# Differential attention scores: three products of rounded parts in place of one fp32 product, from the third step on

## The reference, cut to what matters

```python
dq = rope(rmsnorm(dq.reshape(B, S, DIFF_HEADS, 2, HEAD_DIM), diff_q_norm_g[l]), pos)
dk = rope(rmsnorm(dk.reshape(B, S, DIFF_HEADS, 2, HEAD_DIM), diff_k_norm_g[l]), pos)
...
    s = jnp.einsum('bqhcd,bkhcd->bhcqk', qb, k).astype(jnp.float32) * scale
    causal = kpos[None, :] <= qpos[:, None]
    p = jax.nn.softmax(jnp.where(causal, s, -jnp.inf), axis=-1)
    a = p[:, :, 0] - lam * p[:, :, 1]
    return jnp.einsum('bhqk,bkhe->bqhe', a.astype(v.dtype), v)
```

## Time and profile before

| | us |
|---|---|
| runs | 2419.97, 2422.97, 2423.15 (median 2422.97) |
| profiled execution, its own time | 2423.33 |
| its span in the profile | 2421.6 |
| PE busy | 2408.6 |
| DVE busy | 1426.1 |
| ACT busy | 983.4 |
| POOL busy | 233.9 |

### The profile page before, as it was taken

The page is one execution under the profiler, slowest core; times in us unless marked ns, Lnnn a source line. Parts: engine busy times, 40 slices in busy tenths (PEclk is TensorE's granted clock), DMA queues, the critical chain, the costliest instruction groups (busy, mean ns, idle before and its releaser), DMA issues.

```text
span 2421.6 us, 33933 instructions
## 1 busy us (share of the span) xinstructions
PE 2408.6 (99%) x11896; PEld 1950.9 (81%) x11896; DVE 1426.1 (59%) x2836; ACT 983.4 (41%) x1710; POOL 233.9 (10%) x354
## 2 busy tenths in 40 slices
PE   9999999999999999999999999999999999999999
PEld 7877788888887887888888788788887778888887
DVE  6756436777526447677762579846647864432532
ACT  4333424333323336443331343834336852432331
POOL 0000000000001004000000042301002840000000
PEclk9999999999999999999999999999999999999999
DMA  5322233333322330333333232042222003333333
GB/s 138 87 79 77 80 99 93 95 96 95 121 96 78 95 87 10 99 99 99 95 113 96 89 98 88 19 156 73 85 79 62 1 27 96 92 99 96 96 96 104
DMA packets 278507, 210.95 MB, mean 87 GB/s; under 512 B 12228, under 2 KB 234097, under 8 KB 278385
## 3 DMA queue, kind: packets, MB, share of 16 engines
q1 hardware_dynamic: 270465, 198.64, 27.8%
q10 hardware_dynamic: 7920, 10.70, 1.3%
HBM read 207.22 MB, written 2.10 MB: 86 GB/s over the span
## 4 chain that ended last, share of the span: by engine, by line
PE 88%; DVE 4%; POOL 2%; issue 2%; POOLq 1%; ACT 1%; DVEq 1%; DMA 0%; ACTq 0%
PE PS L161 15%; PE PS L163 15%; PE PS L162 15%; PE PS L158 11%; PE PS L159 11%; PE PS L160 11%; POOL PN L1909 2%; POOLq L1911 1%; DVE WL L154 1%; PE PS L1767 1%; PE PS L1776 1%; PE PS L668 1%; PE PS L1744 1%; PE PS L2435 1%; PE PS L2617 1%
## 5 line engine op out<-in xcount | busy, mean ns | idle before, releaser
L154 DVE TENSOR_TENSOR WL<-RAW,WH 128x1024 fp32r<-128x1024 f32 x352 | 432.8, 1229 | 691.3 <-ACT WH L149 684.1
L149 ACT ACTIVATE WH<-RAW 128x1024 fp32r<-128x1024 f32 x354 | 374.7, 1059 | 963.7 <-PE PS L160 527.2
L161 PE MATMUL PS<-XH,WH 128*128 128x512 f32 x1512 | 593.9, 393 | 0.4 <-DVE WL L575 0.2
L163 PE MATMUL PS<-XH,WL 128*128 128x512 f32 x1512 | 588.7, 389 | 0.0
L162 PE MATMUL PS<-XL,WH 128*128 128x512 f32 x1512 | 588.5, 389 | 0.0
L161 PEld LDWEIGHTS PS<-XH,WH 128*128 128x128 f32 x1512 | 283.9, 188 | 63.9 <-issue 3.3
L163 PEld LDWEIGHTS PS<-XH,WL 128*128 128x128 f32 x1512 | 283.8, 188 | 59.5
L162 PEld LDWEIGHTS PS<-XL,WH 128*128 128x128 f32 x1512 | 284.0, 188 | 58.5 <-issue 1.0
L158 PE MATMUL PS<-WH,XH 128*128 128x512 f32 x384 | 153.2, 399 | 1.1 <-DVE WL L154 1.1
L159 PE MATMUL PS<-WH,XL 128*128 128x512 f32 x384 | 150.5, 392 | 0.0
L160 PE MATMUL PS<-WL,XH 128*128 128x512 f32 x384 | 150.4, 392 | 0.0
(11 more groups left out here) (538 smaller groups left out, 3850.4 us busy)
## 6 DMA issues: line engine op xcount, KB each, us to landing
RAW<-in_ffn_w_up SPq DMA_DIRECT2D x88, 512.0 KB, 3.6
RAW<-in_w_in SPq DMA_DIRECT2D x60, 512.0 KB, 3.6
RAW<-in_ffn_w_down SPq DMA_DIRECT2D x44, 512.0 KB, 3.6
RAW<-in_sc_ssm_w_in SPq DMA_DIRECT2D x42, 512.0 KB, 3.7
RAW<-in_w_mlp_up SPq DMA_DIRECT2D x32, 512.0 KB, 3.9
RAW<-in_w_mlp_down SPq DMA_DIRECT2D x32, 512.0 KB, 3.6
RAW<-in_fox_w_in SPq DMA_DIRECT2D x24, 512.0 KB, 3.6
RAW<-in_sc_ssm_w_out SPq DMA_DIRECT2D x16, 512.0 KB, 3.6
```

Of the source, the lines that this page charges most:

```text
L149: act.activation(WH[:, slot, :], RAW[:, slot, :], ACT.Copy).then_inc(hi_ready, 1)
L154: dve.tensor_tensor(WL[:, slot, :], RAW[:, slot, :], WH[:, slot, :], ALU.subtract).then_inc(lo_ready, 1)
L161: pe.matmul(o, wh, ah, start=first, stop=False)
L163: return pe.matmul(o, wl, ah, start=False, stop=last)
```

## The change

From step t = 2 on, the scores are no longer fp32 products of `DQF` and `DKF` but three fp32r products: (query high, key high), (query low, key high), (query high, key low), the 128-column part included. The parts are made so:

- **Queries, high:** ACT copies tiles 2 to 7 of `DQF` to `DQH`, three after its evictions of unit 19 and three after its work of unit 20.
- **Queries, low:** POOL subtracts, six times 128x512, `DQL` over `DQF`, behind its sixteen pieces of the projection.
- **Keys:** POOL makes the high part with a tensor_scalar and the low part with a tensor_tensor, 128x512 each: for step 2 ahead of its first weights, for steps 3 to 7 each behind the weights of the step three earlier. Three buffers `DKH` take turns; `DKL` lies over `DKF`.
- PE waits ahead of step t for the six low parts of the queries and t-1 of the keys.

```diff
+    def dquery_high_act(act, tiles):
+        act.wait_ge(rd.ev, rd.at.ev + KT)
+        for t in tiles:
+            act.activation(DQH[:, t - 2, :], DQF[:, t, :], ACT.Copy).then_inc(qd.hi, 1)
+
+    def dquery_low_pool(pool):
+        for t in range(2, KT):
+            pool.wait_ge(qd.hi, qd.at.hi + t - 1)
+            pool.tensor_tensor(DQL[:, t, :], DQF[:, t, :], DQH[:, t - 2, :], ALU.subtract).then_inc(qd.lo, 1)
+
+    def dkey_parts_pool(pool, t):
+        pool.wait_ge(rd.ev, rd.at.ev + KT + t + 1)
+        pool.tensor_scalar(DKH[t % 3][:, :], DKF[:, t, :], 1.0, None, ALU.mult)
+        pool.drain()
+        pool.tensor_tensor(DKL[:, t, :], DKF[:, t, :], DKH[t % 3][:, :], ALU.subtract).then_inc(qd.lo, 1)
...
+            if n in (19, 20):
+                dquery_high_act(act, ((2, 3, 4), (5, 6, 7))[n - 19])
...
         for h in range(16):
             dunit_pool(pool, h)
+        dquery_low_pool(pool)
...
+        if t >= 2:
+            if sub == 0:
+                pe.wait_ge(qd.lo, qd.at.lo + DPARTS + t - 1)
+            pair_parts_pe(pe, da, diff_bank(t, sub), t, sub, None, None, diff_parts)
+            return
...
     def diff_pool(pool):
+        dkey_parts_pool(pool, 2)
         for t in range(KT):
...
+            if t + 3 < KT:
+                dkey_parts_pool(pool, t + 3)
```

More of the change, by code:

```diff
@@ L184, in build @@
     ex, w0s, e0, w1s, w2s, e1, w3s = (turn(early_s, half=2 * k, hi=2, lo=2) for k in (1, 0, 1, 0, 0, 1, 0))
+    DPARTS = 6
+    qd = turn(early_s, hi=DPARTS, lo=2 * DPARTS)
     qk = turn(early_s, hi=PARTS, lo=PARTS)
@@ L1721, in pair_parts_pe @@
             n = (qb + 1) * P
-            products = parts(t, qb, n) if qb else ((lambda hh: query(t, hh, qb), lambda hh: key(t, hh, n)),)
+            products = parts(t, qb, n) if qb or query is None else ((lambda hh: query(t, hh, qb), lambda hh: key(t, hh, n)),)
             for m, (q, key_) in enumerate(products):
@@ L2198, in build, with diff_parts, q_high, q_low @@
     rd = turn(rope_s, tab=2, ss=4, rt=4, rope=16, tr=16, ev=16)
+    DQH = a_("DQH", 0, [P, DPARTS, SEQ], F32R)
+    DKH = [a_("DKH0", 12, [P, SEQ], F32R), a_("DKH1", 14, [P, SEQ], F32R), a_("DKH2", 114, [P, SEQ], F32R)]
+    DQL = a_("DQL", 48, [P, KT, SEQ], F32R)
+    DKL = a_("DKL", 64, [P, KT, SEQ], F32R)
+    def dquery_high_act(act, tiles):
[11 more added lines that the diff above has]
+        pool.tensor_tensor(DKL[:, t, :], DKF[:, t, :], DKH[t % 3][:, :], ALU.subtract).then_inc(qd.lo, 1)
+    def diff_parts(t, qb, n):
+        head = [slice(HD * hh, HD * hh + HD) for hh in range(2)]
+        cols = slice(qb * P, (qb + 1) * P)
+        def q_high(hh):
+            return DQH[head[hh], t - 2, cols]
+        def q_low(hh):
+            return DQL[head[hh], t, cols]
+        def k_high(hh):
+            return DKH[t % 3][head[hh], 0:n]
+        def k_low(hh):
+            return DKL[head[hh], t, 0:n]
+        return (q_high, k_high), (q_low, k_high), (q_high, k_low)
     def diff_bank(t, sub):
```

## The result

The changed kernel takes 2432.05 us (median of 6 runs, 2431.19 to 2432.82), the kernel before 2422.23 in the same comparison (6 runs, 2419.97 to 2423.15): a ratio of 1.0043, 95% interval 1.0032 to 1.0054. It is 9.8 us slower. The forecast was 2432.5 in 2424.5 to 2437.

A forecast was written before the change was run, and what follows sets the result against it. It took the path through DVE and ACT to bound up to 1539.51, then PE, DVE and the ACT-DVE loop tied within 0.1 us. Terms 6.0+1.4-0.2+2.0-0 = +9.2 on 2423.3 gave 2432.5 us, range 2424.5 to 2437.

The forecast's parts named there:

- Scores on the path: Scores of steps 2 to 7: PE saves 0.24 to 0.44 us a step, but 0 counted on the path.
- ACT's six copies: ACT's query copies to DQH, the first three behind unit 19's evictions: covered by idle or wider cover, cost 0.
- Query lows: POOL's six query subtractions from about 1498.7 hold DVE's rotations and the ring's low part: 1.00 each, +6.0 us.
- Key parts for step 2: POOL's tensor_scalar and subtraction among the delayed rotations of pieces 13 and 14: 0.4 and 1.0, together +1.4 us.
- What absorbs it: At PE's unit 23 and its scores, waiting for the low part and then the masks: -0.2 us.
- Key parts for steps 3 to 7: POOL's subtraction holds DVE's three combines: 0.5 a period after steps 1 to 4, 0 after step 0; +2.0 us.
- rival C: PE's clock falls in the gap ahead of unit 23, some 3 us more on the path: 2435.5; chance 0.08.
- A: Rival for the stretch 1490 to 1570: POOL's work hidden, PE the bound, only PE's saving left: 2420.7; chance 0.10.
- B: Rival: POOL and DVE collisions at their low end, 3.9 for queries, nothing for keys: +3.7, 2427.0; chance 0.17.
- (1) to (3): Signs: rotations 1499 to 1510 grow about 1 us; ring's low part 6 to 8 later, PE gap 4; first exponential 7 later.
- (5): Sign in the pipeline: period near 6.9 us for steps with key parts and 6.35 without.
- (6): Sign behind 1570: the gap between the two kernels stays constant.

The follow-up runs named there:

- e1: Kernel before with only PE's part: ACT writes tiles 2 to 7 as fp32r, PE makes three products of them, no low parts; 2422.12 us, ratio 1.0000.
- e3: Kernel before, fp32 scores, with only ACT's six query copies added, no POOL subtractions; 2423.03 us, ratio 1.0003.
- e2: Kernel before, fp32 scores, with ACT's six query copies and POOL's six query subtractions added, results unread; 2428.28 us, ratio 1.0030.
- e5: Kernel before, fp32 scores, with ACT's six query copies and six one-input POOL tensor_scalars in place of the subtractions; 2423.54 us, ratio 1.0006.
- e10: Whole changed kernel with the key's high copy written as a tensor_scalar of two operations instead of one; 2430.96 us, ratio 1.0040 to the kernel before.
- e11: Changed kernel with two-operation key copy, six DKH buffers and POOL's subtractions moved to where DVE makes masks; 2425.75 us, ratio 1.0016 to the kernel before.
- e8: Kernel before, fp32 scores, with POOL's key parts added, their subtraction replaced by a second one-input tensor_scalar; 2423.40 us, ratio 1.0009.
- e9: Kernel before, fp32 scores, with POOL's key parts added, unread, the high copy written with two operations; 2425.84 us, ratio 1.0016.
- e4: Kernel before, fp32 scores, with only POOL's key parts added: six one-operation tensor_scalars and six subtractions, unread; 2425.78 us, ratio 1.0017.

## Why the prediction came out right

Point by point, by the shift:

- **Scores on the path: 0 taken, -0.1 us a period measured** (e1: 6.36 to 6.25). Right in kind. The two chains had play of 0.1. PE made a step's scores in 2.25 us instead of 2.56 (in the chain, 1.70 and 0.55 for 1.93 and 0.63), 0.31 less and inside the 0.24 to 0.44 of the forecast. The Trainium skill's four passes of true fp32 (FP8 and Floating Point Precision, TensorE Precision Notes) would make it 0.64; this trace shows half of that.
- **ACT's six copies: 0, measured 0.0** (e3).
- **Query lows: +6.0, measured +5.8** (e2). The step that carried most of the sum was right: a price taken from another two-input POOL instruction against the same rotations, plus the difference in length.
- **Key parts for step 2: +1.4, measured +1.05** (shift 5.8 to 6.87 at the first mask, 1519.49). The subtraction cost 0.9 (L2158 at 1512.98, 1.59 for 0.69), the copy 0.16 and not 0.4, in line with the 0.28 of a one-input read in e5.
- **What absorbs it: -0.2, measured 0.** The scores behind the gap ended 6.87 us late, like the masks.
- **Key parts for steps 3 to 7: +2.0, measured +3.7.** This is the mis-sized term, and it lies above its own bound of 3.2. For the parts made after step 0, where I took 0, it was +1.0; after step 1, 0; after steps 2 to 4, +0.9 each (7.24 instead of 6.36) for my 0.5. The mechanism, the subtraction on the three combines, was right. The size was off because the copy was priced at 0.76 by a tensor_scalar with two operations, and the form with one takes 1.49. That pushed the subtraction 0.7 us later, from half beside the masks to wholly beside the combines. With the short copy (e10) a period grows by 0.57, near my 0.5. For the same reason the forecast's "neither POOL nor PE's wait for the parts is late" was too easy about POOL: the pair needs 1.49+1.48 and two gaps of 0.15 to 0.19, 3.3 us and not 2.25, which is more than the 3.01 that POOL rests in a period.

The sum of the measured terms is 5.8+1.05+0+3.7-0.2 = 10.35 (the -0.2 is from the two periods without key parts), beside 9.2. That the time still came within 0.5 us of the forecast owes something to the base: I counted from a profiled execution at 2423.3, 1.1 above the median of 2422.23 that the six runs of before gave. The terms were 1.15 too low and the base 1.1 too high; that the two cancel is luck.

Two sums of the prediction don't come out. The bounds of its terms add up to +3.7 and +12.7, that is 2427.0 to 2436.0; the 2427.8 to 2435.5 that it calls the bounds are the limit of what can be told from no change and the time of rival C. And collisions under 2.6 us together would be under 0.43 for each of six subtractions, not 0.25. Neither changes which rival is right.

Of the rivals, A (POOL hidden, PE the bound) is refuted by e1 and e2, B (low-end collisions) by e2. C happened in part. The windows of the changed kernel behind the 4.00 us gap, which ends at 1516.02, (columns as in the earlier trace rows):

```profile
1517.00:1520.00 3.00, 3.00 (x9) 2.35 (x8) 2.75 (x4) 0.00 (x0) 0.00 (x0) 0.50 0.59 175
1520.00:1523.00 3.00, 2.11 (x11) 0.79 (x9) 2.34 (x13) 2.17 (x7) 0.35 (x1) 0.97 0.63 175
```

The granted clock was 0.50, the 1.2 GHz level, for the 3 us from 1517 on, about 1 us after the gap had ended, and it was back soon after 1520. But PE then still waited 0.21 and 0.68 us for DVE's masks, so the fall cost nothing here. It would have, had the masks not been just as late. The moment isn't fixed either: in e2, behind a wait of 2.95 us, the clock fell 1.5 us after PE had started again, and in e10, with a wait of 4.16, 1.7 us before, and stayed at 0.50 for 7 us.

Of what was to be seen, (1) to (3) came as written: the rotations beside the subtractions grow by 0.8 to 1.1 us each, the gap is 4.00 us, the first exponential comes at 1520.83, a shift of 6.87. (4) held. (5) was 7.24 for 6.9. (6) held until 1772, where the clock's fall, which differs from one execution to the next, moved the gap by 1.6.

## What to carry to other kernels

Price a GpSimd instruction by what VectorE does beside it, not by its own length: the same subtraction cost 0.97 us beside two-input work and, in the step of e11 shown, nothing beside masks with an operand in PSUM. And price it by a row of exactly the same form, since a neighbouring form of the same operation was twice as fast. Where the chain of waits moves to a new engine, take that engine's length apart from what it does to its neighbours before believing it, as e8 and e9 did together. Ask first what the change could gain if its inputs were free (e1): 0.3 us would have decided this one.

## What the runs showed of the hardware

- A GpSimd tensor_scalar of 128x512 with one operation took 1.49 us, with fp32r and with fp32 output; with two operations (times 1.0 twice) 0.62. The form with more operations was the faster.
- A period with key parts grew by what the three combines were held: 0.47 and 0.46 (e9), 0.59 and 0.57 (e10, against the 6.25 of e1), 1.02 and 1.00 (e4). In e8 it was 0.36 and 0.37, but there POOL's queue was full too.
- Six GpSimd instructions beside VectorE's rotations: memsets 0.0 us, one-input reads 1.7, two-input subtractions 5.8. Both engines lose: the subtractions took 10.24 us (e2) instead of 7.7.
- TensorE's granted clock fell to 0.50 around a wait of about 3 to 4 us in three runs, at a different moment in each: 1 us after the wait for 3 us (changed kernel, wait 4.00), 1.5 us after it for 3.4 us (e2, 2.95), and 1.7 us before its end for 7 us (e10, 4.16).
